# Rounding the weight blocks on GpSimd instead of ScalarE, and starting the modulation transfers from the synchronisation engine

## The reference

```python
def adaln(cond, mod_w, mod_b):
    return jnp.split(jax.nn.silu(cond) @ mod_w + mod_b, 6, axis=-1)

def modulate(h, shift, scale):
    return h * (1 + scale) + shift

def swiglu(h, w_in, w_out):
    g, u = jnp.split(h @ w_in, 2, axis=-1)
    return (jax.nn.silu(g) * u) @ w_out
```

## Time and profile before

| what | value |
|---|---|
| time, median of 3 runs (lowest to highest) | 2477.51 us (2477.03 to 2478.65) |
| the profiled execution: its own time | 2477.56 us |
| its span, first to last instruction | 2475.8 us |
| PE busy | 2444.4 us, 99% |
| DVE busy | 1642.2 us, 66% |
| ACT busy | 1269.5 us, 51% |
| POOL busy | 254.0 us, 10% |
| granted TensorE clock, mean | 0.998 |
| DMA | 485.44 MB, mean 196 GB/s |

### The profile page before, as it was taken

One profiled execution on the slowest core, in us unless ns is written; L12 is line 12 of the kernel. 1 busy time (PEld: TensorE's weight loads), 2 busy tenths in 40 slices (PEclk: granted clock), 3 DMA queues, 4 the chain that ended last, 5 costly groups with the idle time before them and its releaser, 6 DMA issues. The chain is left out here.

```text
span 2475.8 us, 40486 instructions
## 1 busy us (share of the span) xinstructions
PE 2444.4 (99%) x16365; PEld 2138.0 (86%) x16365; DVE 1642.2 (66%) x2431; ACT 1269.5 (51%) x1818; POOL 254.0 (10%) x346
## 2 busy tenths in 40 slices
PE   8999999999999999999999999999999999999999
PEld 8998978889989988977888988798899898766998
DVE  5556786775576566876776657786666656575555
ACT  4444645554444445454554555655556444564443
POOL 1000000111102000000111200220000100152000
PEclk9999999999999999999999999999999999999999
DMA  8755455759968645556656545664356656655654
GB/s 286 241 181 184 149 184 157 281 185 299 270 205 275 196 150 172 177 171 219 241 201 196 190 142 180 190 196 138 119 172 193 205 179 222 195 174 201 197 186 145
DMA packets 240523, 485.44 MB, mean 196 GB/s; under 512 B 17712, under 2 KB 38456, under 8 KB 240272
## 3 DMA queue, kind: packets, MB, share of 16 engines
q1 hardware_dynamic: 215664, 397.07, 50.2%
q0 software_dynamic: 24672, 85.78, 10.7%
HBM read 478.47 MB, written 10.07 MB: 197 GB/s over the span
## 5 line engine op out<-in xcount | busy, mean ns | idle before, releaser
L162 DVE TENSOR_TENSOR wlo<-raw,whi 128x1024 fp32r<-128x1024 f32 (+3 forms) x786 | 915.8, 1173 | 601.5 <-ACT whi L214 600.3
L214 ACT ACTIVATE whi<-raw 128x1024 fp32r<-128x1024 f32 (+3 forms) x786 | 794.5, 1018 | 693.4 <-PE bank L227 644.4
L227 PE MATMUL bank<-xh,whi 128*128 128x256 f32 x2208 | 625.7, 283 | 2.9 <-DVE xl L162 2.5
L227 PE MATMUL bank<-xl,whi 128*128 128x256 f32 x2208 | 620.1, 281 | 0.0
L227 PE MATMUL bank<-xh,wlo 128*128 128x256 f32 x2208 | 620.1, 281 | 0.0
L227 PEld LDWEIGHTS bank<-xh,whi 128*128 128x128 f32 x2208 | 417.0, 189 | 14.7 <-issue 7.5
L227 PEld LDWEIGHTS bank<-xl,whi 128*128 128x128 f32 x2208 | 417.0, 189 | 0.6
L227 PEld LDWEIGHTS bank<-xh,wlo 128*128 128x128 f32 x2208 | 417.0, 189 | 0.0
L227 PE MATMUL bank<-whi,xh 128*128 128x512 f32 (+2 forms) x616 | 246.4, 400 | 3.5 <-DVE xl L162 1.5
L227 PE MATMUL bank<-whi,xl 128*128 128x512 f32 (+2 forms) x616 | 239.1, 388 | 0.0
L227 PE MATMUL bank<-wlo,xh 128*128 128x512 f32 (+2 forms) x616 | 238.9, 388 | 0.0
(11 more groups left out here) (456 smaller groups left out, 3772.6 us busy)
## 6 DMA issues: line engine op xcount, KB each, us to landing
raw<-in_ffn_w_in SPq DMA_DIRECT2D x280, 512.0 KB, 4.4
raw<-in_ffn_w_out SPq DMA_DIRECT2D x154, 512.0 KB, 4.6
raw<-in_w_mix_in SPq DMA_DIRECT2D x112, 512.0 KB, 3.5
store<-in_mod_w POOLq DMA_DIRECT2D x46, 512.0 KB, 8.0
raw<-in_od_w_in SPq DMA_DIRECT2D x40, 512.0 KB, 4.5
stow<-in_mod_w POOLq DMA_DIRECT2D x29, 512.0 KB, 5.1
raw<-in_ffn_w_in SPq DMA_DIRECT2D x56, 256.0 KB, 2.8
raw<-in_w_branch SPq DMA_DIRECT2D x24, 512.0 KB, 3.7
```

Source lines behind the costliest of these rows:

```text
L162: return self.passed(out, self.e and self.e.tensor_tensor(out, a, b, op))
L214: return self.made(us, self.e and self.e.activation(out, a, f, **k))
L227: return self.made(n, self.e and self.e.matmul(out, lhs, rhs, **k))
```

## The change

`whi` is made by GpSimd, with a `tensor_scalar` that multiplies by 1.0 twice, in place of ScalarE's copy. The planner's `fetch()` books it there, at an estimate of its own. The transfers of the modulation weights are started by SP, with twelve semaphores of their own, and the wait for the free tile is SP's too.

```diff
+def load_mod(co, out, in_, free):
+    s = co.s_mod[co.nmod % len(co.s_mod)]
+    co.nmod += 1
+    co.sp.wait_ge(free)
+    if s.n:
+        co.sp.wait_ge(s.mark())
+    co.sp.t = max(co.sp.t, co.pe.t)
+    return co.sp.dma_start(out, in_).then_inc(s, by=16)
...
-    co.ac.wait_ge(landed.mark())
+    co.po.wait_ge(landed.mark())
     if v >= NSPL:
-        co.ac.wait_ge((co.s_use, co.block_of[v - NSPL] + 1))
-    co.ac.activation(hi, raw, ACT.Copy).then_inc(co.s_hi)
+        co.po.wait_ge((co.s_use, co.block_of[v - NSPL] + 1))
+    co.po.scaled(hi, raw, 1.0).then_inc(co.s_hi)
...
-        co.ac.t = max(co.ac.t, co.pe.t, co.fetched) + 0.17 + 0.00086 * n
-        lo = co.dv.t = max(co.dv.t, co.ac.t + 0.1) + 0.15 + 0.00104 * n
+        co.po.t = max(co.po.t, co.pe.t, co.fetched) + 0.2 + 0.00105 * n
+        lo = co.dv.t = max(co.dv.t, co.po.t + 0.1) + 0.15 + 0.00104 * n
...
-        co.po.wait_ge(free)
-        landed = load_small(co, tile[:, :], co.A["mod_w_2"][l][k * P:(k + 1) * P, b * D:(b + 1) * D])
+        landed = load_mod(co, tile[:, :], co.A["mod_w_2"][l][k * P:(k + 1) * P, b * D:(b + 1) * D], free)
```

More of the change, by code:

```diff
@@ L285, in new_core @@
     co.s_par = [sem(f"s_par{i}") for i in range(12)]
-    co.npar = 0
+    co.s_mod = [sem(f"s_mod{i}") for i in range(12)]
+    co.npar = co.nmod = 0
     co.nuse = co.nsplit = 0
@@ L356, in counts @@
     return (pe_mark(co), co.s_dv.mark(), co.s_ac.mark(), co.s_po.mark(),
-            tuple(s.mark() for s in co.s_par if s.n))
+            tuple(s.mark() for s in co.s_par + co.s_mod if s.n))
 def pe_mark(co):
```

## The result

The changed kernel takes 2612.88 us (median of 4 runs, 2608.89 to 2617.41), against 2477.62 for the kernel before: a ratio of 1.0546, 95% interval 1.0533 to 1.0559. That is 135 us slower. The forecast was 2492, with 2520 as the upper end of its range. The direction was right; the size was short by 121 us.

A forecast was written before the change was run, and what follows sets the result against it. PE was taken to bound the kernel, busy 2444.4 of 2475.8 us. From 2477.56, gains of 8.3 off, 21.7 added on GpSimd and 1 on SP gave 2491.96, forecast 2492 us; range 2475 to 2520.

The forecast's parts named there:

- The duration of whi: One whi on GpSimd was taken at 1.15 us, between 1.06 and 1.38.
- In a steady stretch `whi` and `wlo` then need 2.4 of 2.80 us even when they exclude each other: In steady stretches both fit within PE's 2.80 us for a block, so their mutual exclusion was put at no cost.
- cover: For each block, GpSimd may be kept from whi 5.75 us past ScalarE's old start before PE stops.
- port in every block: Rival: whi over 1.58 us makes GpSimd and VectorE too slow even in steady stretches; 2570 at 1.7 us; chance 0.07.
- The list of holds: Places where waits in GpSimd's queue make whi outlast its cover: gate rows, powers, mixers and cross attention; 13.7 us.
- the handovers: After each of 14 holds GpSimd's next whi may shut out the wlo PE awaits: 0 to 16 us, 8 taken.
- the gate rows: Two places where GpSimd waits 6.62 and 5.96 us for a landing: whi 2.2 and 4.2 us late, sum 6.4.
- The powers' shortening: GpSimd's powers get shorter where wlo will stand behind whi; at 1317.43 the 5.26 us become 0.85.
- SP's queue: Weight loads behind pairs of mod_w loads on SP: 1 us, upper end 22; as rival 2513, chance 0.10.
- The load behind it is then issued about 3 to 4 blocks ahead: In the woven part, the load behind a waiting mod_w pair on SP starts 8.4 to 11.2 us ahead, needing 8.0 to 10.6.
- The gains: ScalarE's relief 2.2 us, earlier VectorE results 3, the last norm's stow wait 3.1: 8.3 us in all (5 to 14).
- The last norm's gap: PE's 3.99 us idle, with GpSimd's power behind a stow transfer, was to go, saving 3.1 us.

The follow-up runs named there:

- e1: The kernel before with only whi moved to GpSimd, modulation's transfers left on GpSimd: 2609.73 us, ratio 1.0529.
- e12: The kernel before with powers off GpSimd, plus a GpSimd instruction nobody waits for beside VectorE in 444 blocks: 2516.64 us, ratio 1.0156.
- e6: The kernel before with the powers taken off GpSimd, VectorE taking a minimum in their place: 2480.27 us, ratio 1.0002.
- e5: The kernel of e1 with the powers taken off GpSimd, VectorE taking a minimum in their place: 2542.27 us, ratio 1.0251.
- e9: The kernel of e1 with the 116 whi held behind waits in GpSimd's queue made by ScalarE again: 2527.01 us, ratio 1.0194.
- e10: The kernel of e1 with 116 other whi, evenly spread over those not held, made by ScalarE again: 2590.46 us, ratio 1.0457.
- e2: The kernel before with only modulation's transfers moved to SP, ScalarE still making whi: 2501.28 us, ratio 1.0092.
- e7: The kernel of e1 with VectorE's wlo subtraction replaced by a ScalarE copy of raw: 2488.24 us, ratio 1.0033.

## Why the prediction was wrong, step by step

- **The duration of whi** was right but for 0.1 us (1.15 forecast): the median is 1.05, just under the range's lower end of 1.06.
- **The failed step** is the sentence "In a steady stretch `whi` and `wlo` then need 2.4 of 2.80 us even when they exclude each other: no cost there, cover intact". It is true of a steady stretch, but the sum put 0 for the collisions in all the others too. Where feed-forward blocks follow one another every 2.8 us (2304 to 2420 us before) e1 loses 0.3 us over 41 blocks. What it leaves out is all that VectorE does besides. In the mixers and norms VectorE's own queue leaves no such room, and there a collision goes on to PE. Only e12 against e6 has the collision by itself: 36 us for 444 instructions, some 0.08 us each in the mean. At that rate 786 would cost some 64 us (my estimate) where I had 0. What stays in e5 and e9, 62 and 49 us, is of that size but holds other waits too, and the 116 `whi` that e10 took away gave back 19 us, twice that rate, which stays unexplained. The rival "port in every block" named the mechanism, but its condition, a `whi` over 1.58 us, was the wrong one.
- **The list of holds was too short.** It had 14 places, 13.7 us and 8 for the handovers. At the two places that I worked out best PE's gaps behind the gate rows are 2.34 us (2.2 forecast) and 2.03 (4.2 forecast). The first agrees in part by luck: the waits for the landing were 4.75 and 3.62 us, not 6.62 and 5.96, and the shut-out `wlo` behind them (1.41 and 2.06 us) is part of the gaps. But 116 `whi` of e1 stood over 0.5 us behind another engine's wait, and with what follows them they cost 82 us (e9); the powers' part, by taking all of them off GpSimd, is 69 (e5). The `tbias` transfers alone, not on the list, stopped PE for 2.3 and 5.9 us. The forecast of VectorE being shut out after a hold was right in kind (2.05 and 3.05 us for a `wlo` of 1.22), and "half" of 16 us was far too little, since it counted 14 places.
- **The powers' shortening** was right. Of the powers on `cst` the longest was 5263 ns and the median 1608, and now:

```profile
L151 POOL TENSOR_TENSOR cst<-cst x50: 543/1017/1837, 1337.7 to 2325.2; 128x8 f32<-128x8 f32 x20, 128x2 f32<-128x2 f32 x16, 128x1 f32<-128x1 f32 x6, 128x3 f32<-128x3 f32 x4
```

- **The clock was not in the sum.** The earlier trace rows show PE at 99% and I took PE's work as fixed. It grew by 43.0 us, most of it behind gaps of about 2 us and more.
- **SP's queue** at 1 us was wrong for the move by itself: 22.5 us (e2). The step that failed is "The load behind it is then issued about 3 to 4 blocks ahead". Ahead of the last norm SP stood 15.6 us for a tile, and the load behind it was started 38 us later than in the kernel before. In the changed kernel all that can be told is the 4 us over e1.
- **The gains** (8.3 us) can't be seen as such. The last norm's gap, which was to go, is 3.71 us long in the changed kernel, since the power's input comes late now (the 7.57 us ahead of it are a wait for `rs`), and a second of 3.66 us follows:

```profile
2410.45 1.38 POOL L151 TENSOR_TENSOR rs<-rs,cst 128x1 f32<-128x1 f32 x2 [7.57 <-DVE rs L170]
```
```profile
2411.85 0.33 PE L230 MATMUL bank<-cst,y 128*128 128x128 f32 x1 [3.71 <-DVE y L166]
...
2420.42 0.55 PE L227 MATMUL bank<-xh,whi 128*128 128x256 f32 x1 [3.66 <-DVE xl L162]
```

In short: `whi` on GpSimd makes 131 of the 135 us. Some 70 of them go with the powers, some 80 with the 116 `whi` that stood behind waits, and the collision alone may be worth some 60. These overlap and are no parts that add up: nearly all of it goes when `wlo` leaves VectorE (e7). PE's longer busy time, 42.2 us in e1 (2486.6 against 2444.4), is inside them. Two things stay open: how much of e7's gain is the missing collision and how much VectorE's shorter queue; and what the planner's new order in the woven part does by itself, as no run has that order without the transfers on SP, or both changes in the order of before.

## What to carry to other kernels

When work moves to an idle engine, go through every instruction that waits in its queue, each with the idle time ahead of it (an idle of 44 us ahead of a small transfer is a hold of up to that length for what is put behind it), not through the longest few. The same goes for a queue that starts transfers: one that waits for its tile holds every weight load behind it. When two engines exclude each other, ask not whether the pair fits a block's time but what else the blocked engine must deliver in that stretch. And where PE is 99% busy, a gap of a few us costs its length and then some at the lower clock (after the 5.91 us above, a matmul of 0.40 us took 0.63), so that many small delays that cover still hides are harmless while a few that outlast it are dear.

## What the runs showed of the hardware

- GpSimd can win the on-chip memory several times in a row. In the timeline at 1093.52 above, VectorE's `wlo` was waiting from 1094.62 on, and still GpSimd's next `whi` ran ahead of it. The Trainium skill ("SBUF — State Buffer", Who interferes with whom) says that whoever issues first holds the pair of ports for the whole instruction and the other blocks. The durations agree (1.22 us becomes 2.05 or 3.05). Here the engine that had been waiting was not the next to get it.
- An operation of VectorE with a single large on-chip input can collide too: `y<-y,mv,rs` on 1024 columns went from 827 to 1375 ns. `dsm<-dssc` on 256 doesn't (423 and 420), and neither does `sa<-bank,sa` (685 and 683), whose other input comes from PE's bank.
- Two costs that were each measured alone did not add up: 131 and 22.5 us became 135. With 116 of the held `whi` back on ScalarE and PE's order nearly that of before, the second came back in full, 26 us; whether the holds or the new order had kept it small is not shown.
